# Two transformer blocks on one core: the running state X kept transposed from load to result, and the FFN's down product computed transposed

## The chip, the core and the metric

The kernel runs on one core of a Trainium2 chip. Five engines work side by side on that core, each through its own list of instructions in a fixed order, and they wait for one another only by semaphores: PE (TensorE, matrix products), DVE (VectorE), ACT (ScalarE), POOL (GpSimd) and SP (SyncE, which here only issues DMAs). Matrix products land in PSUM, which has eight banks of 128 x 512 float32; everything else lives in SBUF. The metric is the time of one execution on the device, in microseconds (us). Before the change it was 2089.01 us, the median of 3 runs (2086.91 to 2091.89).

## What is computed

The input x is 256 tokens x 1024 channels, float32. Four layers follow: two of a first kind and two of a second. The parts of each that bear on this change are:

```
first kind (twice):                        second kind (twice):
x = x + 0.5 * ffn(rmsnorm(x) * g1)         x = x + 0.5 * ffn(rmsnorm(x) * g1)
x = x + mixer1(rmsnorm(x) * g2) @ w_out    x = x + mixer2(rmsnorm(x) * g2) @ w_out
x = x + 0.5 * ffn(rmsnorm(x) * g3)         x = x + 0.5 * ffn(rmsnorm(x) * g3)
x = x + sigmoid(rmsnorm(x)*g4 @ w_gate)    x = rmsnorm(x) * post_norm
        * (p @ w_ple)

ffn(h) = (silu(h @ wg) * (h @ wu)) @ wo     wg, wu: 1024 x 2816    wo: 2816 x 1024
rmsnorm(x) = x / sqrt(mean(x*x over the 1024 channels) + 1e-6)
```

So there are eight FFNs. mixer1 is an mLSTM beside a windowed attention, mixer2 a convolution, a pooling and a differential attention; their insides do not change.

## The kernel before, in words

**Float32 products out of three rounded ones.** PE multiplies a rounded format (fp32r). Every operand is therefore held as a high part (rounded) and a low part (the rest), and a product is high x high + high x low + low x high, added in PSUM. ACT makes each high part (`copy` into a tile of type fp32r), DVE each low part (the value minus the high part).

**Weights as a stream of units.** All weights come from HBM in 706 units of up to 128 x 1024 (512 KB), in the order of use. SP loads them into four slots `raw`; for each unit ACT writes `whi` and DVE writes `wlo` (the instruction that the text calls a split) into five slots, three units ahead of PE. The variables `n` and `m` number the states of X: a stage reads state n and writes state m (0 to 14; `LAST` = 14). The order of each engine's work is written out by hand in the functions `tensor`, `scalar`, `vector`, `gpsimd` and `sync`; in a stage, the index k counts its units, and `step(u0 + k)` splits the unit three ahead.

**X before.** X lies with tokens on the partitions: `X[P, 2, 1024]` (t = 0, 1 the token blocks, h = 0, 1 the halves of 512 channels). A product over channels needs it transposed. `turn_x` (L382) transposes one chunk of 128 channels by two PE instructions of 128 x 128, eight chunks and 16 instructions for each n; from PSUM ACT makes the high part times the gain (`high_x`) and DVE the low part (`low_x`) in `XT`. Four chunks are transposed ahead of the last products of the stage before, four (`rest`) after the first unit or job of the new one. The squares for the norm are summed by ACT over 128 x 1024 (L1115).

**FFN before.** 66 units. Unit `gu` (f, half) holds, for 128 of the 2816 hidden columns, four of the eight chunks of wg and wu. For each chunk and each of the two, PE does one pair: weights high as the stationary operand against the 512 columns [X high, X low] (L429), then weights low against the 256 columns of X high (L430). The result is transposed (hidden column x token). After two such units DVE adds the two halves of the bank (`summed`, L1802), multiplies the gate by the row of 1/rms (L1809), ACT does silu, DVE the product (L1816), ACT and DVE the high and low part into `HTh`, `HTl` (L1821), a ring of eight slots. Behind each gu pair with f > 2 stands a down unit of f - 3: here HTh and HTl are the stationary operand and a unit of wo (128 x 1024) moves, three products of 128 x 512 for each of the four (t, h), all four banks 0 to 3 filled over the whole FFN (L357 to L359; in `tail` L402 to L404). At its end DVE adds bank x 0.5/rms into X (`into_x`). The row of 1/rms is made by copying r over 128 columns and two transposes (`turn_r`, L439), ahead of unit k = 6.

**Mixer outputs** end in `tail` and `into_x` in the same way; the gate stage adds a product made by DVE.

## Time and profile before

| | us |
|---|---|
| runs | 2089.01, 2091.89, 2086.91 |
| the profiled execution | 2086.56 |
| its span, first to last instruction | 2084.8 |
| granted TensorE clock | 1.00 of full speed |
| busy in the span: PE | 2064.3 (99%) |
| DVE | 1494.6 (72%) |
| ACT | 1101.6 (53%) |
| POOL | 126.8 (6%) |
| DMA | 182 GB/s on average |

A busy engine is one that has an instruction in flight. Matmuls overlap one another, so that the duration of one (0.40 us) is longer than the distance between two starts (0.23 us); what a matmul costs a busy PE is the distance between starts. Rows of the timeline give a start, a duration, the engine, the line and the tiles; "x8" says that eight like instructions are drawn together, and a bracket the idle time of the engine before the row with what ended it.

### The profile page before, as it was taken

The page shows a single profiled execution, that of the slowest core. Times are in us where ns is not written, and L with a number is a line of the kernel's source. Part 1 is how long each engine was busy: PE and PEld are TensorE (multiplying, and loading weights), DVE is VectorE, ACT ScalarE, POOL GpSimd, SP SyncE. Part 2 cuts the span into 40 slices and gives each one's busy share as a digit, 9 for nine tenths or more (in the row PEclk, how much of TensorE's full clock was granted, in tenths as well). Part 3 has the DMA queues.
Part 4 walks back from the last instruction along what each step waited for, and adds up shares of the span by engine and source line. Part 5 has one row for each costly group of instructions (what it writes and reads, how often), then busy time and mean ns, then how long its engine had stood idle before and what let it go on. Part 6 is the DMA issues. An engine that isn't in the chain of part 4 may idle for free.

```text
span 2084.8 us, 27974 instructions
## 1 busy us (share of the span) xinstructions
PE 2064.3 (99%) x10864; PEld 1752.9 (84%) x10864; DVE 1494.6 (72%) x2257; ACT 1101.6 (53%) x1641; POOL 126.8 (6%) x140
## 2 busy tenths in 40 slices
PE   9999999999999999999999999999999999999998
PEld 8888888888888888888888888878888888878887
DVE  7666667766676666677667766797667766797666
ACT  5444674544554456654445544675444544675443
POOL 1000100000000001000000000150000000160000
PEclk9999999999999999999999999999999999999999
DMA  8655545555555555455555755535555655535553
GB/s 258 192 190 165 189 144 188 187 186 183 187 191 183 185 169 172 150 191 193 188 182 182 242 183 191 172 111 192 191 190 185 202 190 183 172 112 192 192 190 124
DMA packets 105539, 378.82 MB, mean 182 GB/s; under 512 B 12173, under 2 KB 12837, under 8 KB 105152
## 3 DMA queue, kind: packets, MB, share of 16 engines
q1 hardware_dynamic: 102768, 368.95, 53.5%
q0 software_dynamic: 2208, 7.71, 1.3%
q8 instruction: 86, 1.41, 0.3%
q14 instruction: 45, 0.37, 0.1%
q10 hardware_dynamic: 432, 0.39, 0.1%
HBM read 375.73 MB, written 1.27 MB: 181 GB/s over the span
## 4 chain that ended last, share of the span: by engine, by line
PE 92%; DVE 4%; DMA 1%; ACT 1%; issue 1%; POOL 0%; SPq 0%; POOLq 0%; DVEq 0%; ACTq 0%
PE pb L429 31%; PE pb L430 16%; PE pb L357 13%; PE pb L358 13%; PE pb L359 13%; DVE scr L1707 2%; DMA raw<-in_W 1%; DVE wlo L1693 1%; PE pb L382 1%; PE pb L476 1%; PE pb L404 1%; PE pb L402 1%; PE pb L403 1%; PE pb L564 1%; ACT whi L1076 0%
## 5 line engine op out<-in xcount | busy, mean ns | idle before, releaser
L429 PE MATMUL pb<-XT,whi 128*128 128x512 f32 x2816 | 1002.0, 398 | 2.6 <-DVE XT L1707 1.0
L1693 DVE TENSOR_TENSOR wlo<-raw,whi 128x1024 fp32r<-128x1024 f32 (+1 forms) x702 | 848.3, 1216 | 56.0 <-ACT whi L1076 55.8
L1076 ACT ACTIVATE whi<-raw 128x1024 fp32r<-128x1024 f32 (+1 forms) x706 | 730.1, 1045 | 296.1 <-PE pb L430 171.8
L430 PE MATMUL pb<-XT,wlo 128*128 128x256 f32 x2816 | 790.1, 281 | 0.0
L429 PEld LDWEIGHTS pb<-XT,whi 128*128 128x128 f32 x2816 | 529.0, 188 | 132.3 <-issue 1.8
L430 PEld LDWEIGHTS pb<-XT,wlo 128*128 128x128 f32 x2816 | 531.8, 189 | 5.9
L1802 DVE TENSOR_REDUCE sbuf_s<-pb 128x256 f32<-128x512 f32 x240 | 154.5, 686 | 243.8 <-PE pb L430 243.8
L357 PE MATMUL pb<-whi,HTh 128*128 128x512 f32 x816 | 321.0, 393 | 2.3 <-DVE HTl L1821 1.2
L358 PE MATMUL pb<-wlo,HTh 128*128 128x512 f32 x816 | 319.4, 391 | 0.0
L359 PE MATMUL pb<-whi,HTl 128*128 128x512 f32 x816 | 317.8, 389 | 0.0
L1146 ACT ACTIVATE sbuf_s<-sbuf_s 128x256 f32<-128x256 f32 x120 | 49.6, 419 | 348.3 <-DVE sbuf_s L1809 348.2
L357 PE MATMUL pb<-whi,XT 128*128 128x512 f32 (+2 forms) x496 | 189.5, 382 | 0.9 <-DVE scr L1707 0.6
L359 PE MATMUL pb<-whi,XT 128*128 128x512 f32 (+2 forms) x496 | 186.5, 376 | 0.0
L358 PE MATMUL pb<-wlo,XT 128*128 128x512 f32 (+2 forms) x496 | 186.5, 376 | 0.0
L357 PEld LDWEIGHTS pb<-whi,HTh 128*128 128x128 f32 x816 | 153.2, 188 | 37.4 <-issue 3.0
L359 PEld LDWEIGHTS pb<-whi,HTl 128*128 128x128 f32 x816 | 153.3, 188 | 33.4
L358 PEld LDWEIGHTS pb<-wlo,HTh 128*128 128x128 f32 x816 | 153.2, 188 | 25.7
L1802 DVE TENSOR_REDUCE sums<-pb 128x256 f32<-128x512 f32 x112 | 72.1, 686 | 135.1 <-PE pb L430 135.1
L2652 POOL TENSOR_TENSOR st<-st,cst 128x2 f32<-128x2 f32 (+3 forms) x35 | 52.5, 1500 | 1741.2 <-DVE st L1718 1551.6
L357 PEld LDWEIGHTS pb<-whi,XT 128*128 128x128 f32 x496 | 93.2, 188 | 20.0 <-issue 2.3
L1146 ACT ACTIVATE sums<-sums 128x256 f32<-128x256 f32 x56 | 23.4, 419 | 161.5 <-DVE sums L1809 161.5
L359 PEld LDWEIGHTS pb<-whi,XT 128*128 128x128 f32 x496 | 93.2, 188 | 17.2
(231 smaller groups left out, 1505.7 us busy)
## 6 DMA issues: line engine op xcount, KB each, us to landing
raw<-in_W SPq DMA_DIRECT2D x694, 512.0 KB, 4.2
raw<-in_W SPq DMA_DIRECT2D x8, 264.0 KB, 2.9
scr<-in_bc POOLq DMA_DIRECT2D x2, 640.0 KB, 5.3
raw<-in_W SPq DMA_DIRECT2D x4, 256.0 KB, 4.8
scr<-scratch POOLq DMA_DIRECT2D x8, 128.0 KB, 4.4
scr<-mrow POOLq DMA_DIRECT2D x2, 512.0 KB, 5.3
scr<-in_slope POOLq DMA_DIRECT2D x1, 1024.0 KB, 12.1
scr<-in_Pg POOLq DMA_DIRECT2D x1, 1024.0 KB, 15.3
```

What stands on the lines that cost most here:

```text
L357: pe.matmul(o, ah, bh, start=begin and i == 0, stop=False)
L358: pe.matmul(o, ah, bl, start=False, stop=False)
L359: ins = pe.matmul(o, al, bh, start=False, stop=end and done)
L382: ins = pe.transpose(pb[b][:, t * P:(t + 1) * P], X[:, t, c * P:(c + 1) * P], ident[:, :])
L429: pe.matmul(pb[b + j][:, :], h[:, k:k + P], xs, start=c == 0, stop=False)
L430: ins = pe.matmul(pb[b + j][:, 0:S], l[:, k:k + P], xs[:, 0:S], start=False, stop=c == KD - 1)
L1076: return act.activation(o, i, ACT.Copy, scale=scale)
L1146: act.activation(g, g, ACT.Silu).then_inc(*up("silu", s, f))
L1693: dve.tensor_tensor(wlo[u % W_SLOTS][:, 0:c], raw[u % RAW_SLOTS][:, 0:c], whi[u % W_SLOTS][:, 0:c].bitcast(F32), ALU.subtract).then_inc(*u ...
L1707: return dve.scalar_tensor_tensor(out=o, in0=a, scalar=s, in1=b, op0=op0, op1=op1)
L1802: dve.tensor_reduce(sums_of(f)[:, j, :], pb[b + j][:, :].rearrange("p (s t) -> p t s", s=2), AXX, ALU.add).then_inc(*up(name, s, f))
L2652: pool.tensor_tensor(r, v, cst[:, 0:1].to_broadcast([P, n]), ALU.pow).then_inc(*done)
```

## The change

X is kept transposed throughout: `X[P, 8, 256]`, eight chunks of 128 channels by 256 tokens. The host gives x transposed and turns the result back.

- `high_x` and `low_x` read X in SBUF instead of a transposed copy in PSUM. `turn_x` stays only where a mixer or the gate stage gives its product with tokens on the partitions (m = 2, 4, 6, 8, 10, 13): after a mixer ACT first copies the bank to SBUF (`come`), PE transposes it, and DVE adds it to X chunk by chunk (`turned_x`).
- The FFN first does all 44 gate/up units and keeps all 22 chunks of gated values on chip (8 in the X buffer that is free or in HT, 14 in `H2`, which lies over scratch of the mixers). Then follow the 22 down units. They are laid out by output chunk: 22 tiles of 128 x 128 for chunk 0, then for chunk 1, and so on, eight tiles a unit. Each is one pair as in gate/up (weights stationary), accumulated in bank c % 4.
- When chunk c is done, DVE adds the halves of its bank, multiplies by 0.5/rms and adds to X (`down_x`), ACT and DVE make its high and low part for the next stage, ACT squares it.
- The sum of squares: POOL adds the eight squared chunks (`add_squares`), and PE sums over partitions by a product with a column of ones (`norm_sums`, two 128 x 1 products).
- post_norm between the two layers of the second kind is applied to X chunk by chunk while the next FFN's gate/up runs (`post_x`); at the end the result is scaled by a row of 1/rms and stored by four DMAs.

```diff
-        if f > 2:
-            order.append(("o", f - 3, 0))
-    return order + [("o", f, 0) for f in range(NF - 3, NF)]
+    return order + [("o", j, 0) for j in range(NF)]
...
-        X = sb("X", [P, 2, D])
+        X = sb("X", [P, KD, S])
+        squares = sb("squares", [P, 2, S])
+        square_sum = sb("square_sum", [P, S])
...
+            def norm_sums(n):
+                w.wait_ge(*at("one"))
+                w.wait_ge(*at("add", n, KD - 2 if n == LAST else KD - 1))
+                b = sum_bank(n)
+                fill(b)
+                for t in range(2):
+                    cut = slice(t * P, (t + 1) * P)
+                    ins = pe.matmul(pb[b][:, t:t + 1], square_sum[:, cut], one_col[:, :], start=True, stop=n != LAST)
...
+            def down_pair(b, h, l, k, side, begin, end):
+                pe.matmul(pb[b][:, :], h[:, k:k + P], side.rearrange("p s t -> p (s t)"), start=begin, stop=False)
+                return pe.matmul(pb[b][:, 0:S], l[:, k:k + P], side[:, 0, :], start=False, stop=end)
...
+                def down(u, j):
+                    w.wait_ge(*at("lo", u))
+                    for i in range(8):
+                        c, f = divmod(8 * j + i, NF)
+                        b = c % 4
+                        if f == 0:
+                            fill(b)
                         w.wait_ge(*at("hl", s, f))
-                    return ready
+                        ins = down_pair(b, whi[u % W_SLOTS], wlo[u % W_SLOTS], i * P, h_tile(n, f), f == 0, f == NF - 1)
...
-                    if k == 1 and n:
-                        rest(n)
+                    if k == 1 and n in TURNED:
+                        for c in range(4, KD):
+                            turn_x(n, c)
+                    if k == 4:
+                        norm_sums(n)
...
+            def come(m, u):
+                for h in range(2):
+                    for t in range(2):
+                        if (t, h) == (1, 1):
+                            chunks(m, range(4))
+                        w.wait_ge(*ended(u, 2 * h + t))
+                        copy(coming(m, t, h)[0], pb[OB[t][h]][:, :]).then_inc(*up("come", m, t, h))
...
+            def turned_x(n, c):
+                w.wait_ge(*at("xt", n, c))
+                axpy(X[:, c, :], pb[banks_of(n)[c]][:, 0:S], 1.0, X[:, c, :], ALU.mult, ALU.add).then_inc(*up("x", n, c))
+
+            def ends_of(m, u):
+                split(u + AHEAD)
+                split(u + 1 + AHEAD)
+                for c in range(4):
+                    turned_x(m, c)
+                for c in range(4):
+                    low_x(m, c)
...
+                def down_x(c):
+                    t = sums[:, c % 2, :]
+                    w.wait_ge(*chunk_done(m, c))
+                    dve.tensor_reduce(t, pb[c % 4][:, :].rearrange("p (s t) -> p t s", s=2), AXX, ALU.add).then_inc(
+                        *up("csum", m, c))
...
+            def add_squares(n):
+                for c in range(1, KD - 1 if n == LAST else KD):
+                    w.wait_ge(*at("xsq", n, 0))
+                    w.wait_ge(*at("xsq", n, c))
+                    done = one("add", n, c)
+                    pool.tensor_tensor(square_sum[:, :], square_sum[:, :], squares[:, c % 2, :], ALU.add).then_inc(*done)
```

Where PE goes from the first FFN to the first mixer, its list before (L402 to L404 are the tail of the down product, L382 the transposes of X, L357 to L359 the mixer's first job):

```order
L404 MATMUL pb<-whi,HTl 128x512
L382 MATMUL pb<-ident,X 128x128 x8
L402 MATMUL pb<-whi,HTh 128x512
L403 MATMUL pb<-wlo,HTh 128x512
L404 MATMUL pb<-whi,HTl 128x512
L402 MATMUL pb<-whi,HTh 128x512
L403 MATMUL pb<-wlo,HTh 128x512
L404 MATMUL pb<-whi,HTl 128x512
L357 MATMUL pb<-whi,XT 128x512
```

and the same place now (L426 and L427 are the pair of the new down product, L376 to L378 the mixer's first job):

```order
L426 MATMUL pb<-H,whi 128x512
L427 MATMUL pb<-H,wlo 128x256
L426 MATMUL pb<-H,whi 128x512
L427 MATMUL pb<-H,wlo 128x256
L376 MATMUL pb<-whi,XT 128x512
L377 MATMUL pb<-wlo,XT 128x512
L378 MATMUL pb<-whi,XT 128x512
```

The transposes are gone, and the down product ends in pairs instead of threes.

DVE at the end of the first mixer and the start of the next FFN, before (L1693 is a split, the rows X<-pb,X add the banks to X, the rows into XT are `low_x`, L1718 the mean):

```order
L1693 TENSOR_TENSOR wlo<-raw,whi 128x1024 x2
L1707 SCALAR_TENSOR_TENSOR X<-pb,X 128x512 x2
L1707 SCALAR_TENSOR_TENSOR XT<-pb,gcol,XT 128x256 x2
L1707 SCALAR_TENSOR_TENSOR X<-pb,X 128x512 x2
L1707 SCALAR_TENSOR_TENSOR XT<-pb,gcol,XT 128x256 x2
L1693 TENSOR_TENSOR wlo<-raw,whi 128x1024 x2
L1707 SCALAR_TENSOR_TENSOR XT<-pb,gcol,XT 128x256 x4
L1718 TENSOR_SCALAR st<-st 128x2
```

and now:

```order
L1721 TENSOR_TENSOR wlo<-raw,whi 128x1024 x2
L1735 SCALAR_TENSOR_TENSOR X<-pb,X 128x256 x4
L1735 SCALAR_TENSOR_TENSOR HT<-X,gcol,HT 128x256 x4
L1721 TENSOR_TENSOR wlo<-raw,whi 128x1024 x2
L1735 SCALAR_TENSOR_TENSOR X<-pb,X 128x256 x4
L1735 SCALAR_TENSOR_TENSOR HT<-X,gcol,HT 128x256 x4
```

The additions to X now stand between the transposes and the low parts, and they come by chunk. ACT at the same place, now (the three banks copied, then for each chunk its high part and its square, the fourth bank, two splits, the other four chunks):

```order
L1120 ACTIVATE scr<-pb 128x512 x3
L1120 ACTIVATE HT<-X,gcol 128x256
L1155 ACTIVATE square_sum<-X 128x256
L1120 ACTIVATE HT<-X,gcol 128x256
L1155 ACTIVATE squares<-X 128x256
L1120 ACTIVATE HT<-X,gcol 128x256
L1155 ACTIVATE squares<-X 128x256
L1120 ACTIVATE HT<-X,gcol 128x256
L1155 ACTIVATE squares<-X 128x256
L1120 ACTIVATE scr<-pb 128x512
L1120 ACTIVATE whi<-raw 128x1024 x2
L1120 ACTIVATE HT<-X,gcol 128x256
```

Before, the bank copies and the squares by chunk did not stand there.

## Rows read from the trace of the kernel before

**Rows 1.** The page, part 1: busy us, share of the span, instructions.

```profile
PE 2064.3 (99%) x10864; PEld 1752.9 (84%) x10864; DVE 1494.6 (72%) x2257; ACT 1101.6 (53%) x1641; POOL 126.8 (6%) x140
```

**Rows 2.** Timeline of PE in an FFN's middle: start us, duration us, engine, line.

```profile
104.44 0.40 PE L429 MATMUL pb<-XT,whi 128*128 128x512 f32 x1
...
108.68 0.40 PE L429 MATMUL pb<-XT,whi 128*128 128x512 f32 x1
...
109.03 0.40 PE L357 MATMUL pb<-whi,HTh 128*128 128x512 f32 x1
...
111.78 0.39 PE L429 MATMUL pb<-XT,whi 128*128 128x512 f32 x1
```

**Rows 3.** Timeline of PE after the two transposes of turn_r, two FFNs.

```profile
377.93 0.39 PE L429 MATMUL pb<-XT,whi 128*128 128x512 f32 x1
...
382.44 0.39 PE L429 MATMUL pb<-XT,whi 128*128 128x512 f32 x1
...
1630.31 0.40 PE L429 MATMUL pb<-XT,whi 128*128 128x512 f32 x1
...
1634.55 0.40 PE L429 MATMUL pb<-XT,whi 128*128 128x512 f32 x1
```

**Rows 4.** Groups of PE by line (busy us, mean ns), then its timeline at 362 us.

```profile
L382 PE MATMUL pb<-ident,X 128*128 128x128 f32 x224 | 29.4, 273 | 0.0
...
362.00 1.04 PE L382 MATMUL pb<-ident,X 128*128 128x128 f32 x8
362.79 0.48 PE L429 MATMUL pb<-XT,whi 128*128 128x512 f32 x1
363.11 0.28 PE L430 MATMUL pb<-XT,wlo 128*128 128x256 f32 x1
```

**Rows 5.** Timeline of PE, small products without rounding in the first mixer.

```profile
302.59 3.68 PE L564 MATMUL pb<-sbuf_h,scr 128*128 128x64 f32 x32
```

**Rows 6.** Waits of PE: line, whom for, us in total, times, longest.

```profile
PE pb L357 <- DVE HTl L1821: 1.2, 1, 1.2
PE pb L357 <- DVE HTl L1707: 1.0, 2, 0.5
...
PE pb L429 <- DVE sbuf_s L1802: 0.7, 1, 0.7
```

**Rows 7.** Timeline of DVE and ACT, end of first mixer; a bank copy.

```profile
363.02 1.65 DVE L1707 SCALAR_TENSOR_TENSOR XT<-pb,gcol,XT 128x256 fp32r<-128x256 f32 x4
...
362.42 1.57 ACT L1076 ACTIVATE XT<-pb,gcol 128x256 fp32r<-128x256 f32 x4 [1.62 <-PE pb L382]
...
300.18 1.09 ACT L1076 ACTIVATE scr<-pb 128x512 f32<-128x512 f32 x2 [1.09 <-PE pb L476]
```

**Rows 8.** Timeline of DVE and POOL in the first mixer2, two inputs in SBUF.

```profile
1388.82 2.56 POOL L2731 TENSOR_TENSOR scr<-scr 128x256 f32<-128x256 f32 x3 [1.22 <-ACT scr L1076]
...
1388.92 0.97 DVE L1707 SCALAR_TENSOR_TENSOR scr<-scr 128x256 f32<-128x256 f32 x1
...
1391.98 0.47 DVE L1707 SCALAR_TENSOR_TENSOR scr<-scr 128x256 f32<-128x256 f32 x1
```

**Rows 9.** Timeline of DVE behind a pair of gate/up units.

```profile
109.23 1.29 DVE L1802 TENSOR_REDUCE sbuf_s<-pb 128x256 f32<-128x512 f32 x2 [2.63 <-PE pb L430]
110.44 0.41 DVE L1809 TENSOR_TENSOR sbuf_s<-sbuf_s,sbuf_h 128x256 f32<-128x256 f32 x1
110.77 1.22 DVE L1693 TENSOR_TENSOR wlo<-raw,whi 128x1024 fp32r<-128x1024 f32 x1
```

**Rows 10.** Timeline of ACT, high part of weight unit 2.

```profile
12.45 1.06 ACT L1076 ACTIVATE whi<-raw 128x1024 fp32r<-128x1024 f32 x1 [1.59 <-DMA raw<-in_W]
```

**Rows 11.** Timeline of the end, all engines.

```profile
2077.85 0.99 POOL L2652 TENSOR_TENSOR st<-st,cst 128x1 f32<-128x1 f32 x1 [177.14 <-DVE st L1707]
...
2078.35 0.74 DVE L1707 SCALAR_TENSOR_TENSOR X<-pb,st,X 128x512 f32<-128x512 f32 x1
...
2081.57 0.34 SPq L2846 DMA_DIRECT2D out<-scr  x1
```

533 lines of the change are left out of this document (252 added, 281 removed).

## The prediction, made before the changed kernel had run

> **What bounds the kernel now.** I read the page's busy shares first: PE is busy for 2064.3 of 2084.8 us [rows 1], so the order of the day is what each PE instruction costs, not what the other engines do. Next the waits of PE: its longest are 1.2, 1.0 and 0.7 us [rows 6], apart from waits inside the mixers, which the change leaves alone. A cover that thin means that work added on PE is paid in full and that work of DVE and ACT is free until PE waits for it. Third, the timeline of PE, for the distance between starts.
>
> **Pace of the products.** In an FFN's middle, from 104.44 to 108.68 lie 12 pairs: 0.3533 us a pair [rows 2]. The down unit behind them runs from 109.03 to 111.78, 2.75 us for twelve 512-column products, 0.229 each. The columns are the same in the new form (12 x 512 = 8 x 768), but it has 16 instructions for 12. There are two paces of the pair, though. After the two transposes of turn_r in the second FFN, 377.93 to 382.44 holds 13 pairs, 0.3469 us each; in the seventh FFN, 1630.31 to 1634.55, 12 pairs at 0.3533 [rows 3]. Seven of the eight FFNs look like the first case, only the seventh, whose PE had to wait for turn_r's input, like the second. Before, the fast pace ends with unit 7, where the first down unit comes in: behind each of those the pairs start slow again. The changed FFN has nothing but pairs from turn_r (k = 6) to its end, 60 units. I expect the fast pace to hold. By FFN, from turn_r on:
> before: 38 gate/up units at 2.82 (8 x 0.3525, the mean over both units of a period) = 107.2, 18 down units x 2.747 = 49.4, the last four 10.9 (0.2275 a product without pairs between them): 167.5 us;
> after: 60 units x 8 x 0.3468 = 166.5 us. That is -1.1 us each, -8.7 us for eight (unrounded: -8.6 to -8.8).
> At the slow pace it is 60 x 8 x 0.3533 = 169.6, +2.1 each, +16.8 us.
>
> **Transposes of X removed.** 224 instructions on L382 [rows 4]. They stay for n = 2, 4, 6, 8, 10, 13 (96). A group of eight takes 0.79 us (362.00 to 362.79), and the product behind it starts its successor 0.32 later instead of 0.23 [rows 4]: 0.88 us. For n = 1, 3, 5, 7, 9, 11, 12 two groups each go: 14 x 0.88 = -12.3 us. The 16 of n = 0 are counted with the start.
>
> **Sums for the norms added.** 14 times two unrounded 128 x 1 products before the last one. The nearest row, unrounded products of 128 x 64, has 32 in 3.68 us, 0.115 each [rows 5]; with 0.09 of disturbance behind, as for the transposes, 0.32 us, n = 11 double: +4.5 us. Bounds: 0.1 each if only the issue counts (+1.5), 0.6 if the weight loads run alone (+8). They wait for POOL's last addition, which I place 3 us behind the last chunk, while PE arrives 5.5 us (two mixer or gate units) or more behind it. Two more transposes for post_norm: +0.3 us.
>
> **Waits that go.** The 1.2 us for the low part of the first hidden chunk in the fifth FFN, since the down product now starts 38 units later; the two 0.5 us at the gate stages behind transposes that are gone; the 0.7 (with what follows it, 0.9) in the seventh FFN, where DVE multiplied all of X by post_norm [rows 6]: -3.1 us.
>
> **Mixer to FFN (n = 2, 6, 10, 13).** Here the chain gets longer: bank copy (0.55) [rows 7], transpose, addition to X, high part and square on ACT, low part on DVE. From the transposes at 356.92 of the first mixer: DVE's four additions, 0.39 apart as in [rows 7], end at 359.0, and only behind them stand the low parts. PE wants the first at 359.16 and gets it at 359.5; the fourth chunk's at 361.7: unit 0 ends 0.45 us later than before. ACT has then four high parts and four squares behind it (0.39 each), copies the last bank until 361.45, and splits units 3 and 4 until 363.5. DVE follows with its two splits until 364.9, four additions until 366.4, and the low parts of chunks 4 to 7. Before, these were ready from 363.4 on, because nothing but the splits stood in front. PE wants chunk 4 at 366.1.
> Here the squares come in. POOL adds them, 0.85 us each, and a DVE instruction with both inputs in SBUF takes 0.97 us beside such an addition and 0.47 without [rows 8]. low_x has moved from PSUM to SBUF and is of that kind. With low parts 0.85 apart PE ends unit 2 at 370.3 instead of 368.45: +1.85 us a stage, +7.4 us for four. Without contention it would be +1.3 each, with waits for ACT on top 3. The gate stages (n = 4, 8) have two units of PE between, and DVE is rid of its two additions of 0.69 us: +0.15 each, +0.3.
> The Trainium skill, "GPSIMD Engine Reference", section 1, says that GpSimd shares its SBUF interfaces with VectorE and contends with its instructions of two SBUF inputs. By that rule the low parts are slowed here and the splits too; without it the four stages would give +5.2 us. This case's trace agrees, with 0.97 against 0.47 us [rows 8].
>
> **FFN to mixer, gate and FFN.** The last chunk is added to X 1.5 us and its low part is ready 2.4 us behind PE's last pair. It is wanted 5.5 us behind (FFN) or 8.2 (mixer, fourth unit). 0 us.
>
> **DVE in gate/up.** Without down units the period of two units shrinks from 8.39 (2 x 2.82 + 2.75) to 5.55 us, so DVE and ACT lose cover. DVE has two reductions (1.29 together), three instructions of 0.41 and two splits of 1.22 [rows 9]: 4.96 by durations, 4.5 by starts, since they overlap a little. 1 us is left. ACT has two splits of 1.06 [rows 10] and two instructions like DVE's of 0.41. 0 us for PE.
>
> **Start.** No transposes ahead, but the squares stand before the high parts of chunks 4 to 7 on ACT, and POOL slows the low parts. I get units 2 and 3 0.8 to 1 us later and the reduction that frees the bank for unit 4 1.5 us later than before; the weights of unit 2 still come at 12.45 [rows 10]: +1.5 us (0 to +3).
>
> **End.** Before, from DVE's first touch of the last bank to the end of the span: 2084.8 - 2078.35 = 6.45 us, of which 3.25 behind the issue of the last store [rows 11]. Now: halves 0.69, two products 0.41 with 0.1 of handover (1.6), square 0.5, four small products 0.4, mean 0.3, root 0.9 (0.99 in [rows 11]), row 0.3, two transposes 0.45, then four products of 128 x 512 at 0.69 (2.8), store 3.3: 10.6 us. +4.1 us.
>
> **Sum.** -8.7 - 12.3 + 4.5 + 0.3 - 3.1 + 7.4 + 0.3 + 1.5 + 4.1 = -6.0 us on the profiled execution's 2086.56, which is 2.45 below the median of 2089.01. On the median: 2083.0 us.
>
> **Rivals.**
> A. The slow pace, from turn_r to the end in every FFN. This is the case on the other side: +16.8 in place of -8.7, the sum +19.5, 2108.5 us. For it: before, the pairs fall to it behind every down unit, and a wait of PE at turn_r gave it in the seventh FFN. The place is the pair behind turn_r; if the row of 1/rms comes later than PE (I have 0.9 to 1.9 us of room), the FFN runs slow, at 3.2 us each, and from two such FFNs on the gain is gone. Against it: seven of eight. 0.18.
> B. The pace gives nothing: the pairs are fast in gate/up and fall to the slow pace in the down units, where 22 waits for hidden chunks stand between them, or every FFN loses as much as it gains. Sum +2.7, 2091.7 us. 0.16. The Trainium skill, "TensorE: Matmul & The Clock Gate", "Back-to-back issue gap", has N/2.4 + 2.5 ns for a matmul; by that four instructions cost an estimated 2.5 ns more than three for the same columns, some 2 us in all, no pace would change and the time would be about 2093.5. The rows speak against it, since it has 325 ns where they have 347 and 353.
> C. The openings behind mixers cost 4 us instead of 1.85, because ACT's copies and squares delay its splits as well: +8.6, 2091.6 us. For it: ACT has nine more instructions there. Against: the weights are split three units ahead. 0.12.
> D. DVE doesn't keep up in gate/up. From 5.55 us of DVE work per period on, every 0.1 us more costs 18 x 8 x 0.1 = 14 us; at 0.1, 2097. Against: 1 us of room. 0.04.
> The forecast has the remaining 0.50, with a range of its own of 2077 to 2088.
>
> **Numbers.** Runs of this kernel tell 0.2% (4.2 us) from no change, so faster means below 2084.8. The forecast's half puts about 0.38 below, 0.12 within; of B and C a part, where another term is kinder, falls below (0.08) and half within (0.12); A and D and the rest of B and C are slower. Faster 0.46, same 0.24, slower 0.30. Range 2074 to 2104: it takes in B and C, D's first step and A where it holds in six of eight FFNs.
>
> **What would show it.** Pairs on L465/L466 and L426/L427 0.347 us apart from turn_r on (right) or 0.353 (A), or a change between the two lines (B). Waits of PE for the low parts in HT or XT behind mixers of 0.4 and about 1.1 us. No wait of PE for DVE in gate/up. Between DVE's last reduction and the end 10.6 us. Durations of low_x near 0.9 us where POOL adds. I am wrong if PE's pace has a third value, or if a wait appears that is none of these.

## The result, and the profile after

The changed kernel took 2102.8 us (median of four runs, 2098.1 to 2103.2) against 2088.6 us (2086.9 to 2091.9) for the one before on the same chip: a ratio of 1.0067 with a 95% interval of 1.0054 to 1.0080. It is slower by about 14 us; the prediction had 2083.0 and faster. The profiled execution took 2102.7 us, 16.2 more than the profiled one of before.

The page of the changed kernel, part 1, answers to [rows 1]:

```profile
PE 2073.1 (99%) x11512; PEld 1785.2 (85%) x11512; DVE 1612.9 (77%) x2440; ACT 1124.3 (54%) x1733; POOL 223.9 (11%) x252
```

PE is still the engine that sets the time, with 8.8 us more of work. POOL has 97 us more. I cut the span into stages by the starts of PE's instructions. For each FFN (q0 to q7, in order of time) the table has the stretch from its first product to turn_r, and the stretch from there to the first product of the next FFN (us, before / after).

| | first product to turn_r | from there to the next FFN |
|---|---|---|
| q0 | 20.72 / 24.70 | 331.40 / 330.00 |
| q1, q3 (behind mixers) | 17.85, 17.61 / 19.86, 19.87 | 198.48, 198.57 / 196.06, 198.16 |
| q2, q4 (behind gates) | 17.83, 17.83 / 18.85, 18.88 | 331.41, 264.93 / 332.02, 261.95 |
| q5, q7 (behind mixers) | 17.87, 17.87 / 19.97, 19.97 | 168.55, 174.34 / 169.45, 180.29 |
| q6 (behind an FFN) | 18.90 / 17.65 | 263.57 / 265.04 |

The first product comes at 8.2 us and not 7.0. So +1.2 there, +13.3 in the first column, +1.7 in the second (+4.2 of it at the end).

**The pace.** PE's timeline in q1 and q2, each from the start of one unit to the start of the fourth unit behind it, 32 pairs; then in q2's down stage, one column chunk of 22 pairs with its worst pair:

```profile
394.09 0.39 PE L465 MATMUL pb<-HT,whi 128*128 128x512 f32 x1
...
405.18 0.39 PE L465 MATMUL pb<-HT,whi 128*128 128x512 f32 x1
...
609.20 0.40 PE L465 MATMUL pb<-XT,whi 128*128 128x512 f32 x1
...
620.51 0.40 PE L465 MATMUL pb<-XT,whi 128*128 128x512 f32 x1
...
728.48 0.40 PE L426 MATMUL pb<-HT,whi 128*128 128x512 f32 x1
...
731.97 0.42 PE L426 MATMUL pb<-H,whi 128*128 128x512 f32 x1
...
732.36 0.39 PE L426 MATMUL pb<-H,whi 128*128 128x512 f32 x1
...
736.21 0.40 PE L426 MATMUL pb<-HT,whi 128*128 128x512 f32 x1
```

11.09 us for 32 pairs is 0.3466 a pair, 11.31 is 0.3534: the two paces of [rows 3]. But only q0, q1 and q4 have the fast one here. From the pair behind turn_r on each FFN repeats one pattern of starts to its last gate/up unit: 230, 117 ns over and over, or 241, 120, 236, 113, 233, 117. The down stage has a third: 7.73 us for 22 pairs, 0.351. In a column chunk the pairs hold 347 ns on hidden chunks 0 to 7, take 355 and 388 at chunks 8 and 10, and then 350. That is the same in 56 of the 64.

**The openings.** PE's longest waits outside the mixers answer to [rows 6] (L465 is a gate/up product, L420 and L1113 stand at the end):

```profile
PE pb L465 <- DVE XT L1735: 2.7, 3, 0.9
PE pb L465 <- DVE wlo L1728: 2.2, 1, 2.2
PE pb L465 <- DVE sbuf_s L1799: 2.1, 1, 2.1
PE pb L420 <- ACT squares L1155: 2.0, 1, 2.0
PE pb L465 <- DVE HT L1735: 1.9, 2, 1.0
PE pb L1113 <- DVE sbuf_h L1765: 1.4, 1, 1.4
```

Behind the first mixer, the timelines of DVE, POOL and PE (low parts of chunks 4 to 7, additions of squares, the third unit's wait, the norm sums):

```profile
369.42 3.65 DVE L1735 SCALAR_TENSOR_TENSOR HT<-X,gcol,HT 128x256 fp32r<-128x256 f32 x4
...
369.44 3.35 POOL L2693 TENSOR_TENSOR square_sum<-square_sum,squares 128x256 f32<-128x256 f32 x4 [3.86 <-ACT squares L1155]
...
370.59 0.47 PE L465 MATMUL pb<-HT,whi 128*128 128x512 f32 x1 [0.93 <-DVE HT L1735]
...
376.77 0.50 PE L414 MATMUL pb<-one_col,square_sum 128*128 128x1 f32 x4
377.13 0.48 PE L465 MATMUL pb<-HT,whi 128*128 128x512 f32 x1
377.44 0.28 PE L466 MATMUL pb<-HT,wlo 128*128 128x256 f32 x1
```

Four low parts take 3.65 us beside four additions: 0.91 each, near the 0.97 of [rows 8]. The norm sums take 0.36 us to the next start, and that product's successor comes 0.31 later and not 0.23: 0.45 us.

The start, on ACT, PE, POOL and PE again:

```profile
6.37 0.51 ACT L1120 ACTIVATE XT<-X,gcol 128x256 fp32r<-128x256 f32 x1 [3.19 <-DMA gcol<-in_gcol]
...
8.22 0.66 PE L465 MATMUL pb<-XT,whi 128*128 128x512 f32 x1 [2.20 <-DVE wlo L1728]
...
18.36 4.12 POOL L2693 TENSOR_TENSOR square_sum<-square_sum,squares 128x256 f32<-128x256 f32 x4 [1.42 <-ACT squares L1155]
...
22.63 0.58 PE L414 MATMUL pb<-one_col,square_sum 128*128 128x1 f32 x4 [0.23 <-POOL square_sum L2693]
...
26.00 0.77 PE L465 MATMUL pb<-XT,whi 128*128 128x512 f32 x1 [2.06 <-DVE sbuf_s L1799]
...
26.78 0.63 PE L465 MATMUL pb<-XT,whi 128*128 128x512 f32 x1
...
27.42 0.63 PE L465 MATMUL pb<-XT,whi 128*128 128x512 f32 x1
```

The first product is late because ACT's first high part of X waits for the gains (`gcol`) and starts at 6.37 us, where it started at 4.96 before. Four additions then take 4.12 us, the first of them 1.48 beside a split. ACT's squares wait for them (their buffer has two slots), its splits stand behind, DVE's splits behind those, and the reduction that frees the bank for unit 4 behind DVE's.

The last two rows show one more cost. From 25.4 to 28.8 us the granted clock is 0.5 of full speed (1.2 GHz); PE had sat idle for 2.06 us of the time just before. Pairs start 0.64 us apart there, and unit 4 takes 4.14 us. In e4 below the clock is at 1.0 in that place and unit 4 takes 2.85. The clock is also at 0.5 from 8.3 to 11.7 us, behind 3.4 us in which PE was busy for 1.2. The kernel before had 1.0 from 4.4 us on, to its last 1.7 us.

The end answers to [rows 11], PE first, then DVE and SP:

```profile
2092.40 0.38 PE L420 MATMUL pb<-one_col,squares 128*128 128x1 f32 x2 [2.04 <-ACT squares L1155]
...
2094.59 0.69 PE L1113 MATMUL pb<-ident,sbuf_h 128*128 128x128 f32 x2 [1.36 <-DVE sbuf_h L1765]
...
2095.32 2.48 DVE L2649 TENSOR_TENSOR scr<-scr,pb 128x512 f32<-128x512 f32 x4 [0.78 <-PE pb L1113]
...
2096.03 2.17 SPq L2882 DMA_DIRECT2D out<-scr  x4
```

### The profile page after: what moved, and what is told of

Read it like the earlier page. It is cut to its first block, busy times and chain, and to the rows that moved or that the text cites. A ratio compares the mean times of both kernels' runs of the same rounds, so it can differ in the third digit from the quotient of the medians.

```text
span 2100.9 us, 29627 instructions
## 1 busy us (share of the span) xinstructions
PE 2073.1 (99%) x11512; PEld 1785.2 (85%) x11512; DVE 1612.9 (77%) x2440; ACT 1124.3 (54%) x1733; POOL 223.9 (11%) x252
## 4 chain that ended last, share of the span: by engine, by line
PE 91%; DVE 5%; ACT 2%; DMA 1%; issue 1%; POOL 0%; SPq 0%; DVEq 0%; POOLq 0%; ACTq 0%
PE pb L465 30%; PE pb L466 15%; PE pb L426 15%; PE pb L427 8%; PE pb L376 6%; PE pb L378 6%; PE pb L377 6%; DVE scr L1735 2%; DVE wlo L1721 1%; PE pb L524 1%; DMA raw<-in_W 1%; ACT whi L1120 1%; PE pb L612 1%; DVE scr L2382 0%; PE pb L585 0%
## 5 line engine op out<-in xcount | busy, mean ns | idle before, releaser
L465 PE MATMUL pb<-XT,whi 128*128 128x512 f32 x2112 | 749.0, 399 | 7.0 <-DVE XT L1735 2.7
L466 PE MATMUL pb<-XT,wlo 128*128 128x256 f32 x2112 | 593.5, 281 | 0.0
L465 PEld LDWEIGHTS pb<-XT,whi 128*128 128x128 f32 x2112 | 397.6, 188 | 106.4 <-issue 7.2
L426 PE MATMUL pb<-H,whi 128*128 128x512 f32 x896 | 318.9, 395 | 0.0
L427 PE MATMUL pb<-H,wlo 128*128 128x256 f32 x896 | 251.2, 280 | 0.0
L465 PE MATMUL pb<-HT,whi 128*128 128x512 f32 x704 | 248.5, 397 | 1.9 <-DVE HT L1735 1.9
L426 PEld LDWEIGHTS pb<-H,whi 128*128 128x128 f32 x896 | 168.1, 188 | 41.2
L466 PE MATMUL pb<-HT,wlo 128*128 128x256 f32 x704 | 197.3, 280 | 0.0
L376 PE MATMUL pb<-whi,XT 128*128 128x512 f32 (+2 forms) x496 | 189.7, 383 | 0.9 <-DVE scr L1735 0.6
L378 PE MATMUL pb<-whi,XT 128*128 128x512 f32 (+2 forms) x496 | 186.6, 376 | 0.0
L427 PEld LDWEIGHTS pb<-H,wlo 128*128 128x128 f32 x896 | 168.2, 188 | 0.0
L465 PEld LDWEIGHTS pb<-HT,whi 128*128 128x128 f32 x704 | 132.0, 187 | 34.7 <-issue 3.2
L426 PE MATMUL pb<-HT,whi 128*128 128x512 f32 x384 | 135.9, 392 | 0.0
L466 PEld LDWEIGHTS pb<-HT,wlo 128*128 128x128 f32 x704 | 133.0, 189 | 0.0
```

Source lines behind the costliest of these rows:

```text
L376: pe.matmul(o, ah, bh, start=begin and i == 0, stop=False)
L378: ins = pe.matmul(o, al, bh, start=False, stop=end and done)
L426: pe.matmul(pb[b][:, :], h[:, k:k + P], side.rearrange("p s t -> p (s t)"), start=begin, stop=False)
L427: return pe.matmul(pb[b][:, 0:S], l[:, k:k + P], side[:, 0, :], start=False, stop=end)
L465: pe.matmul(pb[b + j][:, :], h[:, k:k + P], xs, start=c == 0, stop=False)
L466: ins = pe.matmul(pb[b + j][:, 0:S], l[:, k:k + P], xs[:, 0:S], start=False, stop=c == KD - 1)
```

## The experiments

Three questions: why the pairs run at one pace or another (e1 to e3, e5, e6, e8, e10 to e13, e15, e16), what the openings cost (e4, e7, e9, e14), and how the two kernels compare with the pace taken out (e17, e18). Ratios are to the kernel before, run on the same chip. Changes are to the changed kernel unless said otherwise.

### e1: H2 on a multiple of 64 bytes

```diff
+        pad = sb("pad", [P, 8])
         feed = ExitStack()
```

> A pad of 32 bytes stands ahead of H2, so that the hidden chunks 8 to 21 begin at a multiple of 64 bytes, as HT, XT and the weights do; nothing else changes. In the changed kernel the down pairs hold 346.7 ns while they read chunks 0 to 7 (HT or XT), are disturbed at chunk 8 (355) and chunk 10 (388), and stay at 350 from there to chunk 21, in 56 of 64 column chunks. Theory 1 (where H2 lies makes the down pairs slow): all down pairs at 347, 117 ns less for each of 64 column chunks, -7.5 us, ratio to the changed kernel 0.9964. Theory 2 (something that goes with the place in the chunk, not with the address, does it: an access to the bank just left, the order of the waits): the pattern 355, 388, 351, 349 stays and the time with it, 2102.8 +- 1.5 us. The gate/up pace isn't touched in either theory, except that its fast and slow cases may fall otherwise.

2100.1 us, ratio 1.0067 (1.0052 to 1.0082). Neither theory. The 355 and 388 were gone, but H2 was now read at 346, 354, 354 and a column chunk took 7733 ns, against 7727. The eight pairs on HT or XT, whose distance had not changed, went from 347.9 to 352.8 in the mean: what a pair costs also hangs on the pairs ahead of it. The address matters for the pattern; this one is no better. The gate/up pairs were fast in six FFNs.

### e2: the norm sums two pairs later

```diff
-                    if k == 4:
-                        norm_sums(n)
...
+                        if (f, half, i) == (2, 0, 0):
+                            norm_sums(n)
```

> The products of the norm sums in each FFN stand two pairs later in unit 4 (14 pairs ahead of turn_r and not 16). Theory 1 (which pace the pairs have after turn_r is set by where in its pattern of three pairs the stream stands at turn_r, and the norm sums start that pattern): another number of the eight FFNs is fast than q0, q1 and q4; each FFN more at the fast pace gives about -2 us (304 gate/up pairs times 6.6 ns). Theory 2 (it hangs on the FFN: its buffer, the stage ahead of it, the clock): the same three are fast and the time stays within 2 us of 2102.8. No other term is expected to move: the row of 1/rms comes 0.7 us later, and PE may wait up to that at turn_r.

2108.4 us, ratio 1.0104 (1.0088 to 1.0121); the profiled execution had a span of 2101.7. Fast were q0, q1, q5 and q7: another set, as theory 1 had it. e1 had six fast ones. So the pattern behind turn_r isn't tied to an FFN. That the two pairs moved it isn't shown: each run has one trace, and executions of one kernel lie 5 us apart (2098.1 to 2103.2 for the changed kernel, 2103.5 to 2108.7 here), as much as two or three FFNs at the other pace.

### e3: high, high, low, low

```diff
                         for j in range(2):
                             k = 256 * i + 128 * j
                             pe.matmul(pb[b + j][:, :], h[:, k:k + P], xs, ...)
+                        for j in range(2):
+                            k = 256 * i + 128 * j
                             ins = pe.matmul(pb[b + j][:, 0:S], l[:, k:k + P], xs[:, 0:S], ...)
```

> In gate/up the four products of one X chunk come as high gate, high up, low gate, low up in place of high, low, high, low. Columns and weight loads are the same. Theory 1 (the pace is a pattern that the order of long and short products falls into): another spacing than 347 or 353 for a pair, and the same in all FFNs; a short product can't hide a weight load of 187 ns behind its 107 ns, two short ones in a row even less, so 2 x 187 + about 2 x 230 = 834 ns for the four, against 694 to 707, is the upper bound (+160 us or so in all); the lower is 694, -10 us. Theory 2 (the pace of loads and columns is a sum, whatever the order): 694 to 707 ns for the four, as now, time within 10 us of 2102.8.

2098.0 us, ratio 1.0054 (1.0039 to 1.0069). Gate/up at 348.3 ns a pair in all eight FFNs; in q2, 32 pairs take 11.15 us:

```profile
610.37 0.40 PE L465 MATMUL pb<-XT,whi 128*128 128x512 f32 x1
...
621.52 0.40 PE L465 MATMUL pb<-XT,whi 128*128 128x512 f32 x1
```

Theory 1: the order has a spacing of its own and only one. The down stage stayed at 351.

### e4: one addition on POOL

```diff
-                for c in range(1, KD - 1 if n == LAST else KD):
+                for c in [KD - 2 if n == LAST else KD - 1]:
```

> Left out: POOL's additions of the squares of chunks 1 to 6 (the norms are taken from two of eight chunks); ACT squares all of them as now. Theory 1 (POOL's additions slow the low parts of X and the splits, and hold up ACT's squares at the start): after a mixer, units 0 to 5 shorter by about 1.3 us each (from +2.1 to +0.8 against before), the start with units 0 to 5 of the first FFN by 2 to 3 us, the end unchanged; in all -7 to -8 us, 2095. Theory 2 (the longer chain of copy, transpose, addition, high part and low part alone makes the openings late, rival C's ACT among it): units 0 to 5 within 0.4 us of what they are, 2102.8 +- 2. The pace of the FFNs is not the object, but may fall otherwise.

2091.9 us, ratio 1.0026 (1.0016 to 1.0035). First product to turn_r: 19.97 in q0, 18.76 to 18.86 behind mixers, 18.0 behind gates; 10.8 us less over the eight, while only q2 and q3 were fast. Theory 1. With the additions go the waits of ACT's squares for them, so e4 doesn't tell the two apart, and of the 4.7 us in q0 1.3 are unit 4, where the granted clock is now 1.0. DVE at the place shown above (low parts of chunks 4 and 5, then 6), and PE's wait:

```profile
366.92 0.87 DVE L1735 SCALAR_TENSOR_TENSOR HT<-X,gcol,HT 128x256 fp32r<-128x256 f32 x2
368.00 0.49 DVE L1735 SCALAR_TENSOR_TENSOR HT<-X,gcol,HT 128x256 fp32r<-128x256 f32 x1 [0.21 <-ACT HT L1120]
...
367.54 0.47 PE L465 MATMUL pb<-HT,whi 128*128 128x512 f32 x1 [0.40 <-DVE HT L1735]
```

### e5: the same order in the down units

```diff
+                        if i % 2 == 0:
+                            for g in (0, 1):
+                                pe.matmul(pb[b][:, :], whi[...][:, (i + g) * P:...], h_tile(n, f + g)..., ...)
+                        ins = pe.matmul(pb[b][:, 0:S], wlo[...][:, i * P:...], h_tile(n, f)[:, 0, :], ...)
```

> The down products of two hidden chunks come as high, high, low, low, all four into the bank of their column chunk; gate/up is left as in the changed kernel. In e3 the same order made gate/up 347.9 ns a pair in all eight FFNs, where high, low, high, low had 346.7 or 353.3. Theory 1 (that order alone makes the spacing, whatever is read): 347.9 a pair in the down units too, 176 x (352.0 - 347.9) = 0.7 us an FFN, -5.8 us; the kick of 388 ns behind chunk 10 is gone with the pattern. Theory 2 (where the hidden chunks 8 to 21 lie, or that all goes into one bank, limits it): 350 and more from chunk 8 on, time within 2 us of 2102.8 but for the lottery of gate/up.

2100.8 us, ratio 1.0064 (1.0044 to 1.0084). The down pairs held 349.6 on chunks 0 to 7 and 353.6 on H2, 352.0 in the mean, against 351.2 in the changed kernel. Theory 2.

### e6: the down units begin with chunk 8

```diff
+def hidden(c, i):
+    return (i + H_SLOTS) % NF if c else i
...
-                        w.wait_ge(*at("hl", s, f))
+                        w.wait_ge(*at("hl", s, hidden(c, f)))
```

> The down products of column chunks 1 to 7 begin with hidden chunk 8 and end with 7 (the weights are laid out to match); column chunk 0 stays in order. Theory 1 (the hidden chunks in H2 are read at another pace than those in HT or XT): 349 to 354 a pair for the first 14 pairs of a column chunk, and the 346.7 for the last 8, or at least another pattern from pair 14 on. Theory 2 (it goes by the place behind the change of bank: fast for 8 pairs, disturbed behind 8 and 10, then 350): the pattern of a column chunk is as in the changed kernel: 357, 346 to 347 seven times, 355, 347, 388, 348, 355 and then 350. In neither does the time change by more than 2 us.

2099.1 us, one run. In column chunks 1 to 7 the pattern had moved with the hidden chunks: 355, 347, 388, 348, 355 and then 350 at the front, 346 to 347 in the last eight pairs. Theory 1: it is the tile that is read.

### e7: squares and additions later

```diff
+                    if k in (2, 3) and (n == 0 or n in TURNED):
+                        for c in range(4 * (k - 2), 4 * (k - 1)):
+                            square_x(n, c)
```

> At the openings of FFNs behind mixers and gates, and in the first FFN, ACT squares chunks 0 to 3 in unit 2 and chunks 4 to 7 in unit 3, behind its splits, and POOL adds them then; nothing is left out. Theory 1 (e4's gain of 10.8 us comes from POOL's additions beside the low parts and from ACT's squares before its splits): nearly all of it is kept, units 0 to 5 at 20.0 us in the first FFN (24.7 in the changed kernel), 18.8 behind mixers (19.9) and 18.0 behind gates (18.9), 2092 +- 3. Theory 2 (the work that is moved only slows the splits and reductions of units 2 to 5, or the sums come late): norm sums wait for the last addition, turn_r waits for the row of 1/rms, units 3 to 5 are longer by what units 0 to 2 gain, 2100 or more.

2127.7 us, ratio 1.0197 (1.0182 to 1.0213). Theory 2. PE's longest wait:

```profile
PE pb L414 <- POOL square_sum L2693: 23.1, 7, 5.4
```

Seven additions took 7.39 us in the opening of q3, the two beside DVE's splits 1.1 and 1.7 us and the others 0.74, so the last one came up to 5.4 us behind the norm sums' place. In five of the openings the granted clock is at 0.5 around that wait, for 3.4 to 10.2 us, which adds to the time.

### e8: the kernel before with high, high, low, low

The edit of e3 in the kernel before.

> The kernel before, with the four products of an X chunk in gate/up as high gate, high up, low gate, low up. Theory 1 (that order holds 347.9 ns a pair wherever it stands): its gate/up pairs, at 346.7 only in units 6 and 7 of seven FFNs and 353.3 else, all go to 347.9, 8 x 38 units x 8 pairs x 5.0 ns = -12 us, ratio 0.994; so the four-instruction pace is no gain of the change. Theory 2 (behind each down unit, with its three products of 512 columns, the pace falls back whatever the order): 350 or more, under -6 us.

2074.3 us, ratio 0.9938 (0.9922 to 0.9955). Theory 1: -13 us where it had -12. From one gate/up unit to the one four further on, two down units between:

```profile
598.56 0.39 PE L429 MATMUL pb<-XT,whi 128*128 128x512 f32 x1
...
615.15 0.39 PE L429 MATMUL pb<-XT,whi 128*128 128x512 f32 x1
```

16.59 us, where two periods of the kernel before take 16.78 (8.39 each, as the prediction has it).

### e9: the sum of squares as one reduction on DVE

```diff
+                    if k == 3 and (n in TURNED or n == 0):
+                        dve.tensor_reduce(square_sum[:, :], sq8[:, :, :].rearrange("p c t -> p t c"), AXX, ALU.add)...
```

> At the openings behind mixers and gates and in the first FFN, ACT's eight squares go to eight slots (the memory of the hidden chunks, free then), DVE sums them by one reduction of 128x2048 in unit 3, and POOL has nothing to add there; the products of the norm sums stand four pairs into unit 4. Nothing is left out. e7, where POOL's additions came later, made PE wait 23.1 us for them in seven FFNs. Theory 1 (the openings are late by POOL's additions beside DVE's work, wherever they stand; ACT's squares cost little): units 0 to 5 as in e4: 20.0 us in the first FFN, 18.8 behind mixers, 18.0 behind gates, 2092 +- 4 in all. Theory 2 (the eight squares on ACT ahead of the splits, or a late sum, are the cost): PE waits at the norm sums or turn_r, units 0 to 5 at 19.9 or more behind mixers, 2100 or more.

2114.7 us, ratio 1.0126 (1.0108 to 1.0143). Theory 2 in its second form: units 0 to 3 were as fast as in e4, and all was given back at the sum.

```profile
1453.03 3.76 DVE L1851 TENSOR_REDUCE square_sum<-sq 128x256 f32<-128x2048 f32 x1
...
1456.85 0.61 PE L418 MATMUL pb<-one_col,square_sum 128*128 128x1 f32 x4 [1.29 <-DVE square_sum L1851]
```

Seven of its FFNs were at the slow pace besides.

### e10: the hidden chunks low in SBUF

The scratch region, H2 with it, is allocated ahead of all other tiles.

> The tiles change places in SBUF: the scratch region with H2 comes first (H2 at 16512 bytes in place of 132576) and all the others behind it (HT at 167168 in place of 73856). In e6 the pattern of the down pairs went with the hidden chunk: 346.7 ns from HT and XT, 349 to 351 from H2 with 355 and 388 at chunks 8 and 10. Theory 1 (what lies high in SBUF is read more slowly): now the H2 chunks go at 346.7 and those of HT or XT at 350, and gate/up, whose X chunks and weights lie high now, doesn't reach 346.7 in any FFN. Theory 2 (H2 is slow for another reason than its place, such as the change from one tile to another in mid-column): the down pattern stays as it is.

2100.2 us, one run. Neither theory: H2 at 351.2 with the pattern of e1, HT and XT at 353.3 or 346.7. Height has no part. What e1 and e10 share is 128 bytes, modulo 256, between H2 and the weights; the addresses themselves leave 0 and 128 (132608 in e1, 16512 in e10), so it isn't the address by itself.

### e11: no norm sums in six FFNs

```diff
-                    if k == 4:
+                    if k == 4 and n in (0, 11):
                         norm_sums(n)
```

> Left out: the products of the norm sums in six of the eight FFNs (all but the first and seventh); DVE takes the mean from a column of the added squares instead. Theory 1 (these two products in unit 4, 16 pairs ahead of turn_r, bring the pairs to turn_r in another part of their pattern, and so make the pace behind it a lottery, while in the kernel before only the transposes 40 pairs ahead did it): these six FFNs are all at 346.7 behind turn_r, as in the kernel before. Theory 2 (the lottery comes from elsewhere, such as the late chunks at the opening): two to four of the six at 353.3.

2100.7 us, one run. DVE takes the mean of these six FFNs from a column of the added squares. q1, q2 and q7 were fast, q3, q4 and q5 slow. Theory 2: the norm sums are not needed for it to fall either way.

### e12: the kernel before with two such products

```diff
+                    if k == 4:
+                        fill(3)
+                        for t in range(2):
+                            pe.matmul(pb[3][:, t:t + 1], ident[:, :], ident[:, 0:1], start=True, stop=True)
```

> The kernel before with two more unrounded products of 128x1 ahead of unit 4 in each FFN, as the changed kernel has them; nothing reads them. Theory 1 (they make the pace behind turn_r a lottery): two to six of its FFNs at 353.3 in units 6 and 7, seven of eight at 346.7 without them. Theory 2: still seven of eight at 346.7. The products themselves cost 8 x 0.45 = 3.6 us, of which nothing hides.

2089.8 us, one run. Three FFNs (q2, q4, q5) had 346.7 behind turn_r, seven without the two products. So these seem enough to upset it, on one trace of each kernel; with e11: the seven of eight that the prediction leaned on were no property of turn_r.

### e13: eight distances

```diff
+        for q, n in enumerate((0, 2, 4, 6, 8, 10, 11, 13)):
+            feed.enter_context(nc.sbuf_tensor(f"skip{n}", [P, 40 + 8 * q], F32))
+            H2[n] = feed.enter_context(nc.sbuf_tensor(f"H2_{n}", [P, NF - H_SLOTS, 2, S], F32R))
```

> H2 begins at another place in each FFN: 0, 32, 64, 96, 128, 160, 192 and 224 bytes (q0 to q7) past a place that has the same remainder by 256 as HT, XT and the weights. So far: remainder the same (HT and XT in the changed kernel, e1 and e6): 346.7 or 353.3 ns a pair; 96 apart (H2 in the changed kernel, e6): 350 with kicks of 355 and 388; 128 apart (H2 in e1 and e10): 346, 354, 354, mean 351.3. Theory 1 (the pattern of the pair hangs on where the operand that is read stands against the weights that are loaded, modulo 256): q0 has 347 or 349, 350, 361 in chunks 8 to 21 as in 0 to 7 and no kick at chunk 10; q3 has 350 or 349, 351, q4 346, 354, 354; the others may show patterns of their own. Theory 2 (it hangs on the tile alone): all eight alike. What it is worth: at 346.7 throughout a down stage of 176 pairs would take 61.0 us and not 61.95.

Theory 1, with eight different results. Column chunk 3 (14 pairs on H2, 8 on HT or XT) took, at 0, 32, ... 224 bytes: 7770, 7640, 7729, 7726, 7733, 7687, 7760 and 7720 ns. The 14 pairs on H2 alone, in the mean of column chunks 1 to 6, took 353.3, 347.2, 352.1, 353.1, 350.7, 347.7, 353.3 and 352.4 ns each: 160 bytes is nearly as good there as 32. Each distance stood in one FFN only. First and last row of column chunk 3 at 0 (q0) and at 32 bytes (q1):

```profile
164.51 0.40 PE L431 MATMUL pb<-HT,whi 128*128 128x512 f32 x1
...
172.28 0.40 PE L431 MATMUL pb<-HT,whi 128*128 128x512 f32 x1
...
516.39 0.39 PE L431 MATMUL pb<-XT,whi 128*128 128x512 f32 x1
...
524.03 0.39 PE L431 MATMUL pb<-XT,whi 128*128 128x512 f32 x1
```

96 bytes gives the kicks of the changed kernel and 128 bytes the pattern of e1, whose H2 stood 256 bytes lower: the pattern comes again after 256 bytes.

### e14: two reductions, and the order of e3

```diff
+                    if k in (2, 3) and (n in TURNED or n == 0):
+                        c0 = 4 * (k - 2)
+                        dve.tensor_reduce((square_sum[:, :], squares[:, 1, :])[k - 2], sq8[:, c0:c0 + 4, :]..., AXX, ALU.add)...
```

> The changed kernel with gate/up in the order high, high, low, low (e3), POOL's additions of the openings replaced by two reductions on DVE of four squares each, in units 2 and 3, ahead of the splits there, and the products of the norm sums four pairs into unit 4; the mean stands ahead of the split of its unit. In e9 one reduction of all eight, 3.76 us, came 1.2 to 1.9 us late in each opening. Theory 1 (the openings cost what POOL's additions and late sums make them cost, and the pace what the order makes it): units 0 to 5 at 20.0, 18.9 behind mixers and 18.1 behind gates, gate/up at 347.9, no wait at the norm sums or turn_r: 2102.8 - 10 - 7 = 2086 +- 3, as fast as the kernel before. Theory 2 (more work on DVE at the opening is as dear as POOL's additions): units 0 to 5 at 19.8 or more behind mixers, 2094 or more.

2103.5 us, ratio 1.0071 (1.0054 to 1.0088). Theory 2: 20.6 us behind mixers, 19.6 behind gates, 26.4 in q0. The sum came in time (longest wait 0.2 us), but with two reductions of 2.0 us DVE was late with what frees a bank for unit 4 (2.6 us in q0) and unit 5. The openings' cost couldn't be taken out without leaving sums out.

### e15: all FFN tiles 32 bytes past

```diff
+        skip = sb("skip", [P, 8])
         HT = sb("HT", [P, H_SLOTS, 2, S], F32R)
...
+        skip2 = sb("skip2", [P, 40])
         feed = ExitStack()
```

> The changed kernel, order high, low as it was, with HT, XT and H2 all beginning 32 bytes past the remainder by 256 that the weights have. In e13 the down pairs that read H2 at that distance held 347.3 ns a pair over whole column chunks, against 351.2 in the changed kernel and 353.2 at distance 0. Theory 1 (the distance between the operand read and the weights loaded sets the pattern, and 32 bytes has one that keeps to 346.7): gate/up and down both at 346.7 to 347.5 in all eight FFNs. Gate/up: five FFNs x 304 pairs x 6.6 ns = -10 us; down: 1408 x 4.5 ns = -6.3 us; 2102.8 - 16 = 2087 +- 3, level with the kernel before (2087.6). Theory 2 (e13's q1 was a lucky phase): three to six FFNs fast, as in every layout so far, and 2097 to 2103.

2096.0 us, ratio 1.0040 (1.0026 to 1.0055). Theory 1 for the pace: every pair, gate/up and down, in all eight FFNs at 346.7 (q2, 32 gate/up pairs and one column chunk of 22):

```profile
609.79 0.39 PE L467 MATMUL pb<-XT,whi 128*128 128x512 f32 x1
...
620.88 0.39 PE L467 MATMUL pb<-XT,whi 128*128 128x512 f32 x1
...
726.96 0.39 PE L428 MATMUL pb<-HT,whi 128*128 128x512 f32 x1
...
734.59 0.39 PE L428 MATMUL pb<-HT,whi 128*128 128x512 f32 x1
```

11.09 and 7.63 us. The time missed its 2087, since the mixers behind q0 and q2 went from 162.6 to 165.8 us each: there X is loaded and the weights are read, and the spacing of their products rose from 227 ns to 233 in the mean (231, 232 and 235 in turn). The gates lost 0.6 us each. The stages behind q4 and q6 lost 0.7 and 2.2; each has 3.4 us at a granted clock of 0.5, which the changed kernel's don't have, so that loss isn't the distance's alone.

### e16: the kernel before, XT 32 bytes past

The same pad ahead of XT.

> The kernel before with XT alone 32 bytes past the remainder of the weights; the hidden tiles stay. Theory 1 (as in e15): its gate/up pairs, 352.9 ns now, at 346.7 to 347.5: 8 x 304 x 5.8 ns = -14 us, ratio 0.993, as much as the order high, high, low, low gave it (e8). Theory 2: 352.9 stays, 2087.6 +- 1.5. In the mixers, where X is the operand that is loaded and the weights are read, the spacing of 0.227 us for 512 columns may change: unknown, up to 1% of 650 us either way.

2080.5 us, ratio 0.9966 (0.9954 to 0.9977). Gate/up periods of 8.30 us and not 8.39, the first two mixers 2.7 us longer each. The kernel before had the same loss.

### e17 and e18: 32 bytes past in the FFNs alone

```diff
+            views = []
+            for at_ in (0, 8):
...
+                views.append(alias.enter_context(nc.sbuf_tensor(f"{name}_{at_}", shape, F32R)))
...
+        HT, HT_ffn = twice("HT", [P, H_SLOTS, 2, S], 4096 + 64)
```

e17, the changed kernel:

> The changed kernel with every tile that FFN pairs read 32 bytes past the weights' remainder, as in e15, while the mixers and gates keep their tiles at the old place (two views of the same memory, 32 bytes apart). e15 had 346.7 in all pairs, but its mixers lost 3.3 us twice and 0.6 us at each gate. Theory 1 (the distance also sets the mixers' pace, where X is loaded and weights are read): mixers back at 162.6 and 28.7 us, 2096.0 - 8 = 2088 +- 2: with the pace that the prediction assumed (0.3468) the changed kernel is level with the one before as it is. Theory 2 (e15's mixers lost for another reason): 2096.

e18, the kernel before with two such views of XT:

> The kernel before with the same: XT 32 bytes past in FFNs alone. e16 won 7 us with XT moved everywhere, of which its first mixers gave back 2.7 each. Theory 1: 2087.4 - 13 = 2074 +- 2, as with the order high, high, low, low (e8). Then the two kernels at one pace differ by 14 us for the changed one, against 2.7 in the prediction's sum without its pace term (rival B), and the rest is start (+3.7), gates (+1), norm sums (+2) and the pace that the old down units never lacked. Theory 2: 2080, and the difference is 8.

e17: 2086.1 us, ratio 0.9995 (0.9986 to 1.0004). e18: 2072.9 us, ratio 0.9935 (0.9923 to 0.9948). Theory 1 for both; the first two mixers are back at 162.6 us in e17 and at 162.9 in e18. From the first pair behind turn_r on an FFN of e17 takes 166.5 us, all eight alike. At one pace the changed kernel is slower by 13 us, and e18 beats both kernels. Its lead over e17 by the two traces (13.4 us of span): first product 0.75 us, first product to turn_r 14.0, from turn_r to the next FFN -5.9, end 4.6. First product and turn_r of q1, in e17 and in e18 (19.81 and 17.58 us apart):

```profile
361.90 0.47 PE L481 MATMUL pb<-HT,whi 128*128 128x512 f32 x1
...
381.71 0.38 PE L491 MATMUL pb<-ident,sbuf_h 128*128 128x128 f32 x2
...
357.93 0.40 PE L444 MATMUL pb<-XT,whi 128*128 128x512 f32 x1
...
375.51 0.38 PE L454 MATMUL pb<-ident,sbuf_h 128*128 128x128 f32 x2
```

## Why the prediction was wrong, step by step

**Pace: the step that failed.** "I expect the fast pace to hold" gave -8.7 us. From the pair behind turn_r to the end of an FFN I had 166.5 us; the trace has 167.3 in q0, q1 and q4 and 169.3 in the other five. Summed, the term is about +8 in place of -8.7, and this alone turns the sign: some 10 us are gate/up at the slow pace in five FFNs, some 6 the down stage at 351 ns. Two errors are in it. The first was to read seven of eight as a property of turn_r: e12 made it three of eight with two tiny products, so rival A's 0.18 looks too little; its pace came in five FFNs. The second was to apply the pace of pairs that read XT to pairs that read H2, a tile at another distance from the weights, for which no row stood: 351 ns in the mean of the 1408 down pairs. That was the place for a bound, and a third value of the pace was the prediction's own sign of being wrong. The mechanism is settled as far as a rule: e13 (eight distances, eight patterns), e15 (32 bytes: 346.7 in every FFN pair) and e17. Why a distance modulo 256 bytes does this, and why distance 0 has two paces that last, stays open. With 346.7 ns in every pair the FFNs of e17 take the 166.5 us assumed.

At the pace assumed the forecast would still have failed: e17 is 1.0 us below the kernel before where the sum has 6.0, and the kernel before gains 14 us from the same edit (e18). Its down units, 2.75 us, were never slower than eight of the best pairs, 2.77.

**Start: +1.5 forecast, about +5 found** (1.2 to the first product, 4.0 behind it, norm sums in it). The chain was named, squares ahead of the high parts and POOL beside the low parts, but not that ACT's squares wait for POOL's additions (0.96, 1.28 and 0.47 us), nor that the granted clock would be at 0.5 behind PE's wait, 1.3 us in unit 4. e4 takes 4.7 us off it, both together.

**Mixer to FFN: right in size, not in its parts.** With the norm sums 2.17 each forecast, 2.0 to 2.3 found. But e4 puts the additions at 1.0 to 1.1, where the term had 0.55 for them (1.85 against 1.3 without contention); the longer chain, without them and the norm sums, costs 0.5 to 0.8 and not 1.3. The two errors cancel, which is luck. The splits, which the prediction expected to be slowed as well, kept their 1.2 us in the changed kernel but for one. e7 and e9 show that moving the sum doesn't help. Rival C's 4 us didn't come.

**Gate to FFN: 0.47 with the norm sums, 1.0 found.** The two units between don't cover POOL's additions, since e4 gains 0.85 there. **Norm sums: 0.32 forecast, 0.45 found**, +2 over fifteen; fifteen times 0.32 is 4.8, and the sum has 4.5. **q6:** up to turn_r the wait and one group of transposes went and two norm sums came, -1.25 us where the terms give -1.14; the second turn of a row costs 1.0 and not 0.3, with 0.6 of it a wait.

**End: +4.1 forecast, +4.2 found. DVE in gate/up:** no wait of PE for it, as forecast. **Transposes:** 96 are left as forecast, and PE's stages without FFN are 0.2 to 1.3 us shorter. With the terms as found (pace 8, start 4.7, mixers 6.7, gates 1.1, norm sums 6.7, second turn of a row 1.0, end 4.2, waits -3.1, transposes -12.3) the sum is about +17 us, against 16.2 between the two profiled executions.

The outcome lies between the rivals: the pace term is +8 where B has 0 and A 16.8, with A's pace in gate/up of five FFNs and a third value in the down units that neither had. 2102.8 us lies inside the range of 2074 to 2104, which was drawn for A in six FFNs; the down stage's third value and the start, which also brought it there, aren't in A. The Trainium skill, "TensorE: Matmul & The Clock Gate", "Back-to-back issue gap", has N/2.4 + 2.5 ns for an isolated matmul; for a pair that is an estimated 325 ns. No run here came below 346.7, and e13 has values from 347 to 353 for the same instructions.

## What to carry to other kernels

A spacing read from the trace belongs to its operands: whoever moves the same products onto another tile has no row for it, and should bound it by the slowest neighbouring row. Where a pattern of starts lasts for hundreds of instructions and another stands beside it, count it as chance until a small disturbance has been tried. In a stream of unlike products on a full PE, two cheap trials are worth it before any restructuring: the order of the products (e8: -13 us) and the distance of the tiles (e18: -14 us). And a wait of PE in an opening is read together with the granted clock behind it, since it may cost more than its own length.
